# The up projection of a ConvFFN by Strassen's scheme, and its down projection as a pass of its own

## The chip, the cores and the metric

The kernel runs on one core of one Trainium2 chip. The metric is the device time of one launch in microseconds (us). Everything is float32 at the boundary: inputs, outputs and the bytes that move. Most large products are made in three passes of a rounded float32 format (fp32r): a value x is split into a rounded part "hi" and a rest "lo" = x - hi, and a product is w_hi·x_hi + w_hi·x_lo + w_lo·x_hi.

## The reference, cut to what matters

One layer of a hybrid decoder serves a prompt (1024 tokens) and a sample group (8 x 4 = 32 tokens), together T = 1056 columns. The part that changes is the last one, the ConvFFN, with D_MODEL = 1024, D_FF = 2816 and a causal depthwise convolution of width 3:

```
x1 = _layer_norm(DN_ALPHA * x + mix, p['ln1_g'], p['ln1_b'])
h, ffn_state = _causal_dwconv(ffn_prev, x1 @ p['w_up'], p['ffn_dw_w'], p['ffn_dw_b'])
hg, hv = jnp.split(h, 2, axis=-1)
f = (jax.nn.silu(hg) * hv) @ p['w_down']
y = _layer_norm(DN_ALPHA * x1 + f, p['ln2_g'], p['ln2_b'])
```

w_up is 1024 x 5632, w_down is 2816 x 1024. The 5632 up columns are 22 gate tiles and 22 value tiles of 128; gate tile q and value tile q make a pair and give inner tile q (128 of the 2816 inner rows). The outputs are y and the last rows that each convolution and cache has to keep.

## The kernel before, in words

Five engines run programs written out by hand, with semaphores between them: TensorE (PE), VectorE (DVE), ScalarE (ACT), GpSimd (POOL) and SyncE (SP, which only issues DMAs). Nothing is scheduled by a planner: the order of the lines in each engine's block is the order of its work.

In the ConvFFN, channels lie on partitions and the 1056 tokens are columns. The tokens x1 stand split in `x1h` and `x1l` (eight tiles of 128 channels). One weight block, 1024 x 128 of w_up or 256 x 512 of w_down, is 512 KB; it goes through a ring: SP loads it into `wraw`, ACT copies it to `whi` rounded (line 1274), POOL makes `wlo` = raw - hi (line 1482), PE uses both. POOL writes 128x1024 per block.

A pair needs two up products. Each one (`product`, line 2197) runs over 8 channel tiles, 3 passes and 3 chunks of 352 tokens: 72 matmuls of 352 columns, all with a weight load of their own, into three PSUM banks (`psa` for the gate, `psb` for the value). ACT copies the sum to SBUF (`ueg`, `uev`, line 1308) and makes four small copies for the 32 sample tokens. DVE convolves (`ffn_conv`): one tensor_scalar and two scalar_tensor_tensor over 1024 prompt columns (lines 2087 and 2090), the same over 32 sample columns. ACT applies SiLU, DVE multiplies (line 2099), ACT and DVE split the inner tile into `fh`, `fl` (lines 1320 and 2105).

The down projection is woven in: after the two up products of a pair, PE takes half of the down columns of the two inner tiles made before (`down`, line 2856): 4 groups of 18 matmuls of 352 columns. DVE adds each group to the residual in SBUF (`down_add`, line 2119), reading PSUM. So 21 pairs of the 22 follow one another, two to a loop step. The last two inner tiles are multiplied the other way round, with the tokens as the stationary operand and 512 down columns moving (line 2900), which gives y with tokens on partitions; the residual is added there by transposes on PE (line 2887), and DVE, ACT and POOL normalise the rows.

Other names: `res` is x1 in full precision; `stg`, `tmp`, `g_ext`, `zbuf` belong to earlier stages and appear below only as examples of an operation.

Of the kernel before, what the change touches and what calls it, by code (L numbers as in the profile page):

```python
# [24 lines left out]
P = 128  # L25
D = 1024
# [36 lines left out]
def program(nc, A, O):  # L63
    ctx = ExitStack()
    with ctx:
# [72 lines left out]
        psx = [ctx.enter_context(nc.psum_tensor(f"ps{n}", [P, 3, 512], F32)) for n in "ab"]  # L138
# [16 lines left out]
        wm_d = dram("wm_d", [D, D])  # L155

# [47 lines left out]
        rr = at("rr", [P, 8], F32, Z + 29856)  # L204
# [58 lines left out]
        fh = [at(f"fh{j}", [P, 2, T], F32R, X0 + 3 * XB + j * 8448) for j in range(2)]  # L263
        fl = [at(f"fl{j}", [P, 2, T], F32R, X0 + 3 * XB + 16896 + j * 8448) for j in range(2)]
# [6 lines left out]
        yrow = [at(f"yrow{j}", [P, D], F32, X0 + XB + j * 4096) for j in range(4)]  # L271
        fout = at("fout", [P, SG + 1, P], F32, U0)
# [12 lines left out]
        x_in = [sem(f"x_rows_in{j}") for j in range(4)]  # L285
# [26 lines left out]
        ga_in = [sem(f"gate_a_in{j}") for j in range(2)]  # L312
        ma_out = [sem(f"merged_a_out{j}") for j in range(2)]
# [9 lines left out]
        orow_out = [sem(f"latent_rows_out{j}") for j in range(2)]  # L323
# [7 lines left out]
        rr_done = sem("row_sum_inverted")  # L331
# [14 lines left out]
        ql_t = sem("w_uk_transposed")  # L346
        ql_r = sem("w_uk_read")
# [42 lines left out]
        l1_a = sem("residual_scaled")  # L390
# [4 lines left out]
        fh_done = sem("ffn_inner_hi_done")  # L395
        fl_done = sem("ffn_inner_lo_done")
        dn_done = sem("down_tile_done")
# [46 lines left out]
        GATE0, VAL0, DOWN0, GATE1, VAL1, DOWN1 = range(6)  # L444
        NG = FT // 2
        PAIRS = (NG - 1) // 2
        assert NG % 2 == 1

        def kinds(g):
            return (GATE0, VAL0, GATE1, VAL1) if g == "first" else (DOWN0, DOWN1) if g == "last" else range(6)  # L450

        def blk(g, kind):

            if g in ("first", "last"):
                n = (N5 if g == "first" else N5 + 4 + 6 * (NG - 1)) + list(kinds(g)).index(kind)
                return n, n
            n = N5 + 4 + kind + 6 * g[1]
            return 12 * g[0] + n, n

        def acc5(g, kind, q, mm=0):  # L460

            if g == "first":
                return U5[q] + (kind == GATE1 or kind == VAL1)
            if g == "last":
                return U5[q] + 2 + 6 * (NG - 1) + (2 if kind == DOWN1 else 0) + mm // 2
            k = {GATE0: 0, VAL0: 0, DOWN0: 1, GATE1: 3, VAL1: 3, DOWN1: 4}[kind] + mm // 2
            return 12 * g[0] + (U5[q] + 2 + 6 * g[1] + k)

        def inner(g, kind):

            t = 1 if kind in (GATE1, VAL1) else 0
            return (t if g == "first" else 4 * g[0] + (2 + 2 * g[1] + t)), t
# [19 lines left out]
        def count(names):  # L492
# [12 lines left out]
                   + " ".join(" ".join(f"h{c}{k}" for k in range(MT)) + f" x{c}5 x{c}7" for c in (1, 2)))  # L505
        PS = count("m0 t0 m1 t1 t2")
        GS = count(" ".join(f"x{c}1 l{c}1 x{c}3 l{c}3 l{c}5 l{c}7" for c in range(3)))
        part3 = lambda c: slice(c * CH, (c + 1) * CH)

        Y_TURN = (0, 1, 2, 3, 4, 5, 6, 7, 8)  # L510
        Y_BY_VECTOR = (8,)
        YV = count(" ".join(f"s{t}0 s{t}1 v{t} a{t} r{t}" + (f" b{t}" if t in Y_BY_VECTOR else "") for t in Y_TURN))

        def y_half(i, n, h):
            b = i % 4
            if b == 1:
# [33 lines left out]
        def _(sp):  # L550
# [148 lines left out]
            def ffn_load(g, kind):  # L699
                n, ns = blk(g, kind)  # L700
                sp.wait_ge(lo_done, n + 1)
                if kind in (DOWN0, DOWN1):
                    cols = slice(0, D // 2) if kind == DOWN0 else slice(D // 2, D)
                    rows_ = slice(FT - 2, FT) if g == "last" else bass.ds(g[0] * 4 + 2 * g[1], 2)
                    dst = wraw[:, ns % RAW, :].rearrange("p (k c) -> p k c", k=2)
                    sp.dma_start(dst, w_dn_v[:, rows_, cols]).then_inc(raw_in[ns % RAW], 16)
                else:
                    t = kind in (GATE1, VAL1)
                    c = (P if t else 0) + (F if kind in (VAL0, VAL1) else 0)
                    cols = slice(c, c + P) if g == "first" else bass.ds(g[0] * (4 * P) + (c + 2 * P * (1 + g[1])), P)  # L710
                    sp.dma_start(slot3(wraw, ns), w_up_v[:, :, cols]).then_inc(raw_in[ns % RAW], 16)

            for kind in (GATE1, VAL1):
                ffn_load("first", kind)
            with sp.Fori(0, PAIRS) as i:
                for s in range(2):
                    for kind in range(6):
                        ffn_load((i, s), kind)
            for kind in kinds("last"):
                ffn_load("last", kind)  # L720
            sp.wait_ge(h_chain, 12 * FT + 12)
            sp.wait_ge(se_set, 2 * FT)
            sp.dma_start(g2[:, :], A["ln2_g"].to_broadcast([P, D])).then_inc(gb2_in, 16)
            sp.dma_start(b2[:, :], A["ln2_b"].to_broadcast([P, D])).then_inc(gb2_in, 16)
            sp.dma_start(O["conv_s"][0, :, 0:HALO - NT, :], A["state_conv"][0, :, NT:, :]).then_inc(out_s, 16)

            for g in range(SG):
                sp.wait_ge(kf_r, 1 if g < 4 else 2)
                sp.dma_start(state_rows_of(O["ffn_s"][0], g), fout[0:srows(g), g, :]).then_inc(ffn_out, 16)
            sp.dma_start(O["ffn_p"][0, 0].rearrange("t (f p) -> f t p", p=P), fout[0:2 * FT * (FW - 1), SG, :]  # L730
                         ).then_inc(ffn_out, 16)
# [2233 lines left out]
```

## Time and profile before

| | |
|---|---|
| runs | 2050.41, 2047.93 and 2049.80 us, median 2049.8 |
| profiled execution, first to last instruction (span) | 2046.5 us |
| PE busy | 2006.5 us, 98% |
| DVE, ACT, POOL busy | 60%, 35%, 28% |
| granted TensorE clock | 0.997 of 2.4 GHz on average |
| bytes moved | 182.45 MB, 89 GB/s over the span |

The profile gives the span of its execution and not its whole time; the 3.3 us between the span and the median of the runs lie around the instructions. Matmul durations in the rows are latencies that overlap: what a matmul costs is the distance from its start to the next one's start. The ConvFFN begins at about 1254 us and ends with the span.

### The profile page before, as it was taken

To read this page: it belongs to the slowest core of one execution; us is meant where nothing else is said; L and a number is where in the kernel's file an instruction comes from. 1 tells how busy PE (TensorE), PEld (TensorE's weight loads), DVE (VectorE), ACT (ScalarE), POOL (GpSimd) and SP (SyncE) were. 2 spreads that over 40 slices of the span, in tenths; PEclk is the share of its full clock that TensorE was granted. 3 is DMA by queue.
4 is the path that set the end of the run, shared out by engine and by line. 5 is a ranking of instruction groups with operands and counts; after the bars stand their busy time and mean duration, and the time that the engine had idled before them with its cause. 6 is when DMAs were issued, how large, how long until landed. Compare 5 with 4: busy or idle time off the path is not lost.

```text
span 2046.5 us, 33717 instructions
## 1 busy us (share of the span) xinstructions
PE 2006.5 (98%) x13380; PEld 1905.5 (93%) x13380; DVE 1228.7 (60%) x1686; ACT 706.4 (35%) x1175; POOL 564.4 (28%) x284
## 2 busy tenths in 40 slices
PE   8999999999999999989999999999999999999998
PEld 8999999999988999866669998999999999999996
DVE  3999999946755666545453237754545454545447
ACT  4222222226237677653342114322222222222223
POOL 4712444302101010134302256222221212222224
PEclk9999999999999999999999999999999999999999
DMA  6422233215420000166534422111111111111103
GB/s 222 151 94 69 88 95 114 83 53 195 134 74 23 16 23 7 63 233 265 224 148 135 137 90 63 52 46 48 35 58 32 52 42 52 42 52 42 52 31 130
DMA packets 157662, 182.45 MB, mean 89 GB/s; under 512 B 13518, under 2 KB 130528, under 8 KB 153422
## 3 DMA queue, kind: packets, MB, share of 16 engines
q1 hardware_dynamic: 139744, 107.90, 17.3%
q0 software_dynamic: 8320, 46.27, 5.8%
q10 hardware_dynamic: 9469, 26.36, 3.4%
q8 instruction: 106, 1.74, 0.4%
q14 instruction: 23, 0.18, 0.0%
HBM read 149.43 MB, written 31.93 MB: 89 GB/s over the span
## 4 chain that ended last, share of the span: by engine, by line
PE 90%; DVE 5%; ACT 2%; issue 1%; ACTq 0%; DMA 0%; POOL 0%; DVEq 0%
PE psb L2197 28%; PE psa L2197 28%; PE psb L2856 6%; PE psa L2856 6%; PE psb L2390 4%; PE psa L2390 4%; PE pst L2469 1%; PE psb L2657 1%; PE pst L2636 1%; PE psa L2604 1%; PE psb L2604 1%; PE pst L2639 1%; PE psa L2206 1%; PE psb L2343 1%; PE psa L2900 1%
## 5 line engine op out<-in xcount | busy, mean ns | idle before, releaser
L1482 POOL TENSOR_TENSOR wlo<-wraw,whi 128x1024 fp32r<-128x1024 f32 x64 | 172.6, 2710 | 561.5 <-ACT whi L1274 561.5
L1584 DVE SCALAR_TENSOR_TENSOR pst<-g_ext,wtap,pst 128x512 f32<-128x512 f32 x464 | 306.9, 748 | 0.0
L1352 POOL TENSOR_TENSOR wlo<-wraw,whi 128x1024 fp32r<-128x1024 f32 x64 | 154.9, 2425 | 381.5 <-ACT whi L756 286.6
L2087 DVE TENSOR_SCALAR hg<-ueg,fwv,vec 128x1024 f32<-128x1024 f32 x22 | 20.7, 940 | 229.6 <-ACT ueg L1308 225.3
L2197 PE MATMUL psa<-x1h,whi 128*128 128x352 f32 x504 | 109.1, 324 | 0.0
L2197 PE MATMUL psb<-x1h,whi 128*128 128x352 f32 x504 | 109.0, 324 | 0.0
L2197 PE MATMUL psb<-x1h,wlo 128*128 128x352 f32 x504 | 108.6, 323 | 0.0
L2197 PE MATMUL psa<-x1h,wlo 128*128 128x352 f32 x504 | 108.6, 323 | 0.0
L2197 PE MATMUL psb<-x1l,whi 128*128 128x352 f32 x504 | 108.5, 323 | 0.0
L2197 PE MATMUL psa<-x1l,whi 128*128 128x352 f32 x504 | 108.5, 323 | 0.0
L2090 DVE SCALAR_TENSOR_TENSOR hg<-ueg,fwv,hg 128x1024 f32<-128x1024 f32 x44 | 96.9, 2203 | 5.7 <-DVE hg L2087 0.2
L1308 ACT ACTIVATE ueg<-psa 128x1056 f32<-128x1056 f32 x22 | 23.2, 1053 | 219.1 <-PE psa L2197 216.2
L2197 PE MATMUL psa<-xh,whi 128*128 128x352 f32 x432 | 93.6, 325 | 1.2 <-ACT stat L850 1.2
L2197 PE MATMUL psb<-xh,whi 128*128 128x352 f32 x432 | 93.6, 325 | 0.0
L2197 PE MATMUL psb<-xh,wlo 128*128 128x352 f32 x432 | 93.1, 323 | 0.0
L2197 PE MATMUL psa<-xh,wlo 128*128 128x352 f32 x432 | 93.1, 323 | 0.0
L2197 PE MATMUL psa<-xl,whi 128*128 128x352 f32 x432 | 93.0, 323 | 0.0
L2197 PE MATMUL psb<-xl,whi 128*128 128x352 f32 x432 | 93.0, 323 | 0.0
L1428 POOL TENSOR_TENSOR wlo<-wraw,whi 128x1024 fp32r<-128x1024 f32 (+1 forms) x12 | 24.2, 2032 | 245.9 <-ACT whi L934 245.9
L2197 PEld LDWEIGHTS psb<-x1h,wlo 128*128 128x128 f32 x504 | 86.6, 188 | 0.0
L2197 PEld LDWEIGHTS psa<-x1h,wlo 128*128 128x128 f32 x504 | 86.5, 188 | 0.0
L2197 PEld LDWEIGHTS psa<-x1h,whi 128*128 128x128 f32 x504 | 85.8, 189 | 0.3 <-issue 0.3
(550 smaller groups left out, 5249.3 us busy)
## 6 DMA issues: line engine op xcount, KB each, us to landing
wraw<-in_w_up SPq DMA_DIRECT2D x44, 512.0 KB, 3.7
wraw<-in_w_in SPq DMA_DIRECT2D x37, 512.0 KB, 3.8
wraw<-in_w_down SPq DMA_DIRECT2D x22, 512.0 KB, 3.2
xt_d<-tmp POOLq DMA_DIRECT2D x8, 528.0 KB, 3.5
gb_d<-stg ACTq DMA_DIRECT2D x8, 528.0 KB, 2.6
ga_d<-stg ACTq DMA_DIRECT2D x8, 528.0 KB, 3.9
ma_d<-stg ACTq DMA_DIRECT2D x8, 528.0 KB, 2.9
tmp<-gb_d SPq DMA_DIRECT2D x8, 528.0 KB, 3.8
```

Source lines behind the costliest of these rows:

```text
L1308: nc.scalar.activation(split(ue[v][:, FW - 1:]), acc(v), ACT.Copy).then_inc(free[v], 1)
L1352: nc.gpsimd.tensor_tensor(wlo[:, n % HL, :], wraw[:, n % RAW, :], whi[:, n % HL, :].bitcast(F32), ALU.subtract).then_inc(lo_done, 1)
L1428: nc.gpsimd.tensor_tensor(wlo[:, n % HL, 0:w], wraw[:, v, 0:w], whi[:, n % HL, 0:w].bitcast(F32), ALU.subtract).then_inc(lo_done, 1 + s)
L1482: nc.gpsimd.tensor_tensor(wlo[:, (ns + 2) % HL, :], wraw[:, (ns + 2) % RAW, :], whi[:, (ns + 2) % HL, :].bitcast(F32), ALU.subtract).then_ ...
L1584: half[x] = link(nc.vector.scalar_tensor_tensor(out=dst, in0=src, scalar=tap(k_), in1=pst[:, x, :], op0=ALU.mult, op1=ALU.add))
L2087: nc.vector.tensor_scalar(h, src, tap(0), bias, ALU.mult, ALU.add).then_inc(h_chain, 1)
L2090: nc.vector.scalar_tensor_tensor(out=h, in0=src, scalar=tap(k), in1=h, op0=ALU.mult, op1=ALU.add).then_inc(h_chain, 1)
L2197: last = nc.tensor.matmul(out[:, c, 0:CH], w[:, k, :], x[:, k, c * CH:(c + 1) * CH], start=(k == 0 and x is hi_x and w is wh), stop=(k == ...
L2206: last = nc.tensor.matmul(psx[0][:, c, 0:CH], w[:, k, :], x[:, k, part3(c)], start=(k == 0 and x is xh and w is wh), stop=(k == KT - 1 and ...
L2390: r = nc.tensor.matmul(out, w, x, start=first and k == 0, stop=last and k == len(steps) - 1)
L2604: last = nc.tensor.transpose(dst[:, k, v * P:(v + 1) * P], cb[j][:, 4 * g + v, k * P:(k + 1) * P], ident[:, :])
L2856: last = nc.tensor.matmul(psx[q][:, c, 0:CH], w[:, k, cols], x[:, k, c * CH:(c + 1) * CH], start=k == 0 and w is wh and x is fh[p_], stop= ...
```

## The change: what it does

**Up projection.** Pairs 0 and 1 stay as they were. For the other 20 pairs the product of a pair is taken as a 2 x 2 block product: channels in a lower and an upper half (4 tiles each), tokens in a left and a right half (528 each), and as the other side the gate and the value tile. Strassen's scheme in Winograd's form makes it with 7 block products instead of 8, from sums of weight blocks and sums of token blocks:

- Token sums: four blocks of 128 x 4 x 528, made once before pair 2, by DVE (`token_sum`, 8 instructions of 128x1056), split by ACT (`token_high`, 8), DVE and POOL (`token_low`, 4 each). Two of them overwrite `res`, which is first stored to DRAM (`xr_d`, 4.3 MB); DVE's first token sum waits for that store.
- Weight sums: POOL makes four of 128x512 per pair (`up_sum`); ACT and POOL split seven blocks of 128x512 per pair (`up_high`, `up_low`). Raw weights lie in two buffers of four blocks; `whi` and `wlo` have one slot of 512 columns for each of the seven.
- Products: per pair 7 groups of 24 matmuls of 264 columns (`up_product`), into a ring of four places of two PSUM banks. A product waits until the product four before it has been read.
- Results: ACT copies the first product (`first_part`), DVE makes seven additions of 128x528, each of one product in PSUM and one operand in SBUF (`up_add`), and writes gate and value halves straight into `ueg` and `uev`. The big copies of ACT are gone.

**Down projection.** The finished inner tiles go to DRAM (`f_d`). After the last up product, three rounds over the tokens (tiles 0, 1 and the sample; 2 to 4; 5 to 7) run over all 22 inner tiles with the tokens stationary and 512 down columns moving, all by `down_step`; the y rows stay in PSUM for the round. w_down is loaded and split again in every round (66 blocks of 128x1024). The 32 sample tokens are multiplied unsplit in plain float32, four products side by side in four column groups (`sample_step`, 11 times). The convolution of the last pair and its product lie on DVE in the first round. The loops of the ConvFFN are written out.

The core of the diff ("..." where it is cut):

```
-            def ffn_hi(g, kind):
...
+            def up_sum(i, s, out, a, b, op):
+                pool.wait_ge(raw_in[i % 2], UP_IN0 + 64 * (i // 2 + 1))
+                pool.wait_ge(up_s, 4 * i + s - 1)
+                nc.gpsimd.tensor_tensor(out, a, b, op).then_inc(up_s, 1)
+
+            def up_low(i, e):
+                pool.wait_ge(hi_done, UP_HI0 + 7 * i + e + 1)
+                src = sums[:, :] if e == 3 else up_raw(i)[:, (0, 1, 0, None, 2, 1, 3)[e], :]
+                nc.gpsimd.tensor_tensor(wl8[:, UP_SLOT[e], :], src, wh8[:, UP_SLOT[e], :].bitcast(F32), ALU.subtract
+                                        ).then_inc(lo_done, 1)
...
+            def token_sum(n):
+                if n != 1:
+                    dve.wait_ge(xr_out, 32)
...
+                    nc.vector.tensor_tensor(t_sum[n][:, ks, :], a[:, ks, :], b[:, ks, :], ALU.subtract).then_inc(l1_v, 1)
...
+            token_sum(0)
+            token_sum(1)
+            conv(0, 0)
+            token_sum(3)
+            token_sum(2)
+            token_low(0)
+            conv(0, 1)
+            inner(0)
+            token_low(2)
+            for i in range(NP):
+                conv(i + 1, 0)
+                gate_left(i)
+                conv(i + 1, 1, i)
+                inner(i + 1)
+                with_fifth(i)
+                with_seventh(i)
+                value_right(i)
+                if i == NP - 1:
+                    for x in range(4):
+                        inner_low(x)
+                gate_right(i)
+                value_left(i)
+            residual_scale(0)
...
+            def up_product(i, e, dst, hi_x, lo_x):
+                wh, wl = entry(wh8, e), entry(wl8, e)
+                pe.wait_ge(lo_done, UP_LO0 + 7 * i + e + 1)
+                for k in range(HK):
+                    for w, x in ((wh, hi_x), (wh, lo_x), (wl, hi_x)):
+                        for c in range(2):
+                            last = nc.tensor.matmul(dst[:, c, :], w[:, k, :], x[:, k, c * QF:(c + 1) * QF],
+                                                    start=k == 0 and w is wh and x is hi_x,
+                                                    stop=k == HK - 1 and w is wl)
+                last.then_inc(w_used, 1)
...
+            def down_step(r, t, k, hs=(0, 1), stop=False):
...
+                for f, w in ((x1h, whi), (x1h, wlo), (x1l, whi)):
+                    for h in hs:
+                        last = nc.tensor.matmul(y_half(t, h), f[:, x % FR, cols], w[:, s, h * 512:(h + 1) * 512],
+                                                start=False, stop=stop and f is x1l)
```

Where instructions move on DVE: in the steady part, before, the end of a pair, behind the value convolution (`hv` and `hg` are the convolved tiles, `uev` the value tile, `sev` its sample part, `psa` and `psb` PSUM).

```order
L2119 TENSOR_TENSOR res<-res,psb 128x1056
L2098 REGISTER_ALU
L2099 TENSOR_TENSOR hv<-hg,hv 128x1056
L2114 REGISTER_ALU
L2119 TENSOR_TENSOR res<-res,psa 128x1056
L2105 TENSOR_TENSOR fl_198<-hv,fh_196 128x1056
L2116 REGISTER_ALU
L2119 TENSOR_TENSOR res<-res,psb 128x1056
```

In the changed kernel DVE from the value convolution of one of the 20 Strassen pairs to the pair's end (`ps6` and `pst` are PSUM, `u1`, `u3` and `inr` hold partial sums in SBUF).

```order
L2317 TENSOR_SCALAR hv_201<-uev_199,fwv_54,vec_52 128x1024
L2320 SCALAR_TENSOR_TENSOR hv_201<-uev_199,fwv_54,hv_201 128x1024
L2338 TENSOR_TENSOR u1_210<-ps6,u1_210 128x528
L2320 SCALAR_TENSOR_TENSOR hv_201<-uev_199,fwv_54,hv_201 128x1024
L2317 TENSOR_SCALAR hv_201<-sev_203,fwv_54,vec_52 128x32
L2320 SCALAR_TENSOR_TENSOR hv_201<-sev_203,fwv_54,hv_201 128x32 x2
L2328 TENSOR_TENSOR hv_201<-hg_200,hv_201 128x1056
L2338 TENSOR_TENSOR u3_211<-pst,u1_210 128x528
L2338 TENSOR_TENSOR inr_197<-ps6,u1_210 128x528
L2338 TENSOR_TENSOR uev_199<-pst,inr_197 128x528
L2338 TENSOR_TENSOR ueg_198<-ps6,u3_211 128x528
L2338 TENSOR_TENSOR uev_199<-ps6,inr_197 128x528
```

The four additions of down groups and the split of the inner tile have left the pair; seven additions of half the width have come in, five of them at its end, where the third of these five frees the PSUM place that PE's next pair begins with.

POOL before, for three blocks of the ring (a pair takes three: gate, value, down):

```order
L1482 TENSOR_TENSOR wlo_60<-wraw_58,whi_59 128x1024
L1481 REGISTER_ALU
L1482 TENSOR_TENSOR wlo_60<-wraw_58,whi_59 128x1024
L1481 REGISTER_ALU
L1482 TENSOR_TENSOR wlo_60<-wraw_58,whi_59 128x1024
```

POOL in the changed kernel, one pair (the raw weights of every other pair lie in `x1f`):

```order
L1681 TENSOR_TENSOR sums_209<-x1f_196 128x512
L1686 TENSOR_TENSOR wlo_60<-x1f_196,whi_59 128x512
L1681 TENSOR_TENSOR x1f_196<-x1f_196 128x512
L1686 TENSOR_TENSOR wlo_60<-x1f_196,whi_59 128x512
L1681 TENSOR_TENSOR x1f_196<-sums_209,x1f_196 128x512
L1686 TENSOR_TENSOR wlo_60<-x1f_196,whi_59 128x512
L1686 TENSOR_TENSOR wlo_60<-sums_209,whi_59 128x512
L1681 TENSOR_TENSOR x1f_196<-x1f_196 128x512
L1686 TENSOR_TENSOR wlo_60<-x1f_196,whi_59 128x512 x3
```

Three instructions of 128x1024 per pair have become eleven of 128x512.

## Rows read from the trace of the kernel before

**Rows 1.** The page, busy time, share of the span, instructions.
```profile
PE 2006.5 (98%) x13380; PEld 1905.5 (93%) x13380; DVE 1228.7 (60%) x1686; ACT 706.4 (35%) x1175; POOL 564.4 (28%) x284
```
**Rows 2.** The page, the chain that ended last, by engine.
```profile
PE 90%; DVE 5%; ACT 2%; issue 1%; ACTq 0%; DMA 0%; POOL 0%; DVEq 0%
```
**Rows 3.** The chain in order of time: start us, us, what.
```profile
1281.30 11.88 PE psa L2197 x72
...
1747.66 2.91 PE psa L2856 x18
```
**Rows 4.** Timeline of PE, start and duration us: 512 columns, then 256.
```profile
599.28 0.39 PE L2390 MATMUL psa<-ckvh,wlo 128*128 128x512 f32 x1
...
601.36 0.39 PE L2390 MATMUL psa<-ckvh,wlo 128*128 128x512 f32 x1
...
606.01 0.28 PE L2390 MATMUL psb<-whi,ckvl 128*128 128x256 f32 x1
...
607.08 0.28 PE L2390 MATMUL psb<-whi,ckvl 128*128 128x256 f32 x1
```
**Rows 5.** Timeline of PE: plain float32 in four column groups; transposes.
```profile
922.85 1.92 PE L2636 MATMUL pst<-ct,qc 128*32 128x512 f32 x16
...
2004.64 0.60 PE L2887 MATMUL psa<-ident,res 128*128 128x128 f32 x4
2005.00 0.48 PE L2900 MATMUL psa<-whi,fh 128*128 128x512 f32 x1
```
**Rows 6.** One pair of the steady part: us, busy us of each engine, clock, DMA.
```profile
1339.79:1374.74 34.95, 34.95 (x218) 34.95 (x217) 17.20 (x18) 8.12 (x16) 8.12 (x4) 1.00 0.15 46
```
**Rows 7.** Timeline of DVE, start and duration us, one value convolution and what follows.
```profile
1539.18 0.81 DVE L2087 TENSOR_SCALAR hv<-uev,fwv,vec 128x1024 f32<-128x1024 f32 x1 [5.15 <-ACT uev L1308]
1540.12 1.28 DVE L2090 SCALAR_TENSOR_TENSOR hv<-uev,fwv,hv 128x1024 f32<-128x1024 f32 x1
1541.32 1.25 DVE L2119 TENSOR_TENSOR res<-res,psa 128x1056 f32<-128x1056 f32 x1
1542.49 1.28 DVE L2090 SCALAR_TENSOR_TENSOR hv<-uev,fwv,hv 128x1024 f32<-128x1024 f32 x1
1543.68 0.29 DVE L2087 TENSOR_SCALAR hv<-sev,fwv,vec 128x32 f32<-128x32 f32 x1
1544.01 0.54 DVE L2090 SCALAR_TENSOR_TENSOR hv<-sev,fwv,hv 128x32 f32<-128x32 f32 x2
1544.47 1.25 DVE L2119 TENSOR_TENSOR res<-res,psb 128x1056 f32<-128x1056 f32 x1
1545.63 1.25 DVE L2099 TENSOR_TENSOR hv<-hg,hv 128x1056 f32<-128x1056 f32 x1
1546.80 1.25 DVE L2119 TENSOR_TENSOR res<-res,psa 128x1056 f32<-128x1056 f32 x1
```
**Rows 8.** Timelines of DVE and POOL where both work.
```profile
1528.63 4.62 DVE L2090 SCALAR_TENSOR_TENSOR hg<-ueg,fwv,hg 128x1024 f32<-128x1024 f32 x2
...
1528.89 3.27 POOL L1482 TENSOR_TENSOR wlo<-wraw,whi 128x1024 fp32r<-128x1024 f32 x1 [9.93 <-ACT whi L1274]
```
**Rows 9.** Single lines of DVE: duration ns min/median/max.
```profile
L2090 DVE SCALAR_TENSOR_TENSOR hg<-ueg,fwv,hg x44: 1283/1286/3298, 1282.5 to 1984.5; 128x1024 f32<-128x1024 f32 x44
...
L2119 DVE TENSOR_TENSOR res<-res,psb x40: 1246/1252/1255, 1334.7 to 2004.1; 128x1056 f32<-128x1056 f32 x40
...
L1563 DVE COPY gs_ext<-g_ext x8: 181/181/2341, 49.2 to 379.2; 128x32 f32<-128x32 f32 x8
```
**Rows 10.** Groups of POOL's instructions, one of 512 columns: busy us, mean ns.
```profile
L1428 POOL TENSOR_TENSOR wlo<-wraw,whi 128x512 fp32r<-128x512 f32 x4 | 5.2, 1297 | 0.0
```
**Rows 11.** DMA issues of an earlier stage: KB each, us to landing.
```profile
zbuf<-z_d SPq DMA_DIRECT2D x1, 2640.0 KB, 12.4
```
**Rows 12.** Timelines of POOL and PE: last split before pair 1; last matmul.
```profile
1276.73 2.80 POOL L1500 TENSOR_TENSOR x1l<-res,x1h 128x352 fp32r<-128x352 f32 x3
...
2037.45 0.40 PE L2900 MATMUL psa<-whi,fl 128*32 128x512 f32 x1
```

More of the change, by code:

```diff
@@ L439, in program, with wait_used @@
         U5 = list(uses)
[L444 to L472, printed above, removed]
+        Y_END = (4, 12)
+        def wait_used(eng, x):
+            r, k = (x - 1) // FT, (x - 1) % FT
+            if k == FT - 1:
+                eng.wait_ge(y_t, Y_END[r])
+            else:
+                eng.wait_ge(w_used, DN_P0 + r * (FT - 1) + k + 1)
+        up_block = lambda q, v: N5 + 2 * q + v
+        up_free = lambda q, v: U5[v] + q
         w_in_v = A["w_in"].rearrange("l (k p) c -> p (l k) c", p=P)
@@ L713, in _ @@
[L713 to L731, printed above, removed]
@@ L1322, in _ @@
-            act_ffn("first")
-            with act.Fori(0, PAIRS) as i:
-                for s in range(2):
-                    act_ffn((i, s))
+            hi(up_block(1, 1))
+            for k in (0, 2, 4, 6):
+                act.wait_ge(l1_v, VS[f"l2{k}"])
+                step(f"z{k}", nc.scalar.activation(res[:, k, :], res[:, k, :], ACT.Identity,
+                                                   bias=vec[:, V_L1B + k:V_L1B + k + 1]))
+            act.wait_ge(l1_s, AS["z6"])
+            act.wait_ge(l1_g, GS["l27"])
@@ L1346, in _ @@
+            for i in (6, 7, 8):
+                y_scale(i)
         @block.gpsimd
@@ L1525, in _ @@
+            for i in (6, 7):
+                y_bias(i)
         @block.vector
@@ L2091, in ffn_conv, with inner @@
                                                            op1=ALU.add).then_inc(h_chain, 1)
-                        if v and g != "first" and part_ == 0 and k == 1:
-                            down_add(g, DOWN0 if kind == VAL0 else DOWN1, 0)
-            def ffn_mult(g, kind):
-                q, t = inner(g, kind)
+                        if between is not None and part_ == 0 and k == 1:
+                            first_and_sixth(between)
+            def inner(q):
                 dve.wait_ge(si_done, q + 1)
@@ L2807, in first_up @@
             def first_up():
-                blocks = [blk("first", kind) for kind in (GATE0, VAL0)]
+                blocks = [(up_block(0, v), up_block(0, v)) for v in range(2)]
                 for c in range(3):
```

814 lines of the change are left out of this document (544 added, 270 removed).

## The prediction, made before the changed kernel was run
> **What bounds the kernel now.** I read the page first: PE is busy 98% of the span, no other engine over 60% [rows 1], and the chain that ended last runs through PE for 90% [rows 2]. The chain in order of time then shows the ConvFFN as products end to end: 72 matmuls in 11.65 to 11.88 us, 18 in 2.91 [rows 3]. One pair lasts 34.95 us, PE busy for all of it, DVE 17.20, ACT 8.12, POOL 8.12, granted clock 1.00, so the 2.4 GHz level [rows 6]. So PE's matmul starts are the time today, and what counts is whether they still are once the pair is short.
>
> **What PE gains.** The cost of a matmul is the distance of starts. For 512 columns that is (601.36 - 599.28) / 9 = 0.231 us, for 256 it is (607.08 - 606.01) / 9 = 0.119 [rows 4]; the line between them gives 0.161 for 352 columns, and 34.95 / 216 = 0.162 is what a pair shows [rows 6]. So 264 columns cost 0.1225 by the line; the block products change bank at every matmul, as the 352 ones do, and those lie 1 ns over it: I take 0.124 (bounds 0.119 and 0.130). A Strassen pair is 7 x 24 = 168 matmuls, 20.8 us (20.0 to 21.8), where the two products took 144 x 0.162 = 23.3. On PE alone that is 2.5 us a pair, 50 us for 20 pairs.
>
> **The down projection changes little.** Before: 20 pairs x (34.95 - 23.3) = 233 us woven in, and from 2003.9, where the last group ends, to the last matmul's end at 2037.85 another 34 [rows 5, 12]: 267 us. After: 8 whole token tiles x 22 x 3 x 2 = 1056 matmuls of 512 columns at 0.232 are 245; 64 transposes at 0.36 for four [rows 5] are 5.8, and 0.6 for eight first matmuls behind them; the sample is 11 groups of four plain float32 matmuls side by side, of which two took 1.92 us [rows 5], so 10.6; its end and the turned state rows about 3.4. Together 265 us. The second half of the question is therefore DVE, POOL and the two seams.
>
> **DVE and POOL in a steady pair.** DVE's own work, start to start [rows 7]: a convolution 0.94 + 1.20 + 1.19 + 0.33 + 0.46 = 4.12, two of them 8.24, the product of the inner tile 1.17, and seven additions of 528 columns. The addition of 1056 costs 1.17; half of that and the fixed part is 0.62, seven are 4.3. Sum 13.7 us, well under 20.8. POOL: eleven instructions of 512 columns at 1.30 [rows 10], 14.3 us, also under.
>
> But the two don't run freely beside each other. In [rows 8] two scalar_tensor_tensor took 4.62 us instead of the 2.48 that they take alone, while POOL's split between them took 3.27. The longest of their kind took 3298 ns where the median is 1286 [rows 9]: the first ran through, POOL stood until it was done, then the second stood until POOL was done. They take turns, whole instruction by whole instruction. The additions that read PSUM are never touched: 40 of them lie between 1246 and 1255 ns [rows 9], though POOL splits three blocks in every pair [rows 6]. A copy of 32 columns, 181 ns, was held for 2341 [rows 9], so small ones stand in the queue as well.
>
> In a Strassen pair DVE has 13 instructions that read SBUF alone: per convolution one tensor_scalar and two scalar_tensor_tensor of 1024 columns and the same three of 32, and the product. POOL has eleven, and before it had three. As long as POOL has work, DVE waits before each of its 13 for one of POOL's, 1.30 less the 0.2 to 0.3 that an instruction needs to begin anyway: about 1.04. Some of POOL's eleven pass under additions or while DVE waits for PE. I count ten that are waited for: 13.7 + 10.4 = 24.1 us. With eight it is 22.0, with eleven 25.1. PE cannot run ahead, since its next pair begins in the place that DVE's fifth-last work frees (`value_right`), behind all 13. So the pair is the longer of 20.8 and this sum. I take 23.5, a little under 24.1, for the chances of POOL to slip through; range 20.8 to 25.1. That is the size of the 23.3 that it replaces: the gain of PE goes into turns at the port.
>
> The Trainium skill, page "SBUF — State Buffer", section "Who interferes with whom", puts it as an exclusive lock: a DVE instruction with two SBUF inputs, or a two-port mode, and a GpSimd instruction that reads SBUF block each other for the whole instruction, PSUM readers are free. This trace agrees as far as it goes (3298 against 1286 ns, and 1255 at most for PSUM readers); that it also holds for scalar_tensor_tensor of 32 columns no row shows. By the rule the pair is 24.1; if only those four small ones of a pair were free it would be about 21, which is the second case below.
>
> **The seam at the start.** Up to the end of pair 1's product nothing is moved, except four small ACT additions: it ends at 1304.8 (two products behind 1281.30 [rows 3]). The store of `res`, 4.3 MB, can be issued after POOL's last split at 1279.5 [rows 12], some 3 us later with ACT's work. A load of 2.64 MB took 12.4 us [rows 11]; at that rate 4.3 MB take 20 us; nothing else of size moves then, so I take 16, landed at 1299 (1294 to 1304). From there DVE must do, before the second Strassen pair can begin: eight token sums and four splits of 1056 columns (12 x 1.17 = 14.0), four convolutions (16.5), two products (2.3), five additions (3.1): 36 us. POOL has 11 + 11 small ones and four splits of 1056 columns in that time, and about 20 of DVE's 40 turns are lost to them: 21 us. So the second Strassen pair begins at 1299 + 36 + 21 = 1356, say 1355. On PE's account it would be 1304.8 + 20.8 = 1325.6. The seam costs 29 us (10 if DVE never waits for POOL, 34 if the store is late).
>
> **The seam in the middle and the end.** After the last block product DVE has four splits of inner tiles, two additions and the residual scaling (2304 columns, 1.8 us) before PE's first transposes: 5 us if PE was the slower, 8 if DVE was. In round 0 PE needs 3.25 us a step, POOL's split of 1024 columns 2.4, and DVE's last pair is still to be convolved between them: another 4 us. The tail behind the last matmul was 8.65 us; the last tile now has 128 rows and not 32, so 0.7 more for its store.
>
> **The sum** (places on the scale of the profiled execution, whose own time before is its span of 2046.5 and some 3.3 us around it, which makes the median 2049.8): 1355 + 18 x 23.5 + 20.8 for the last pair = 1798.8; + 8 + 4 + 265 + 9.35 = 2085.2, and 3.3 around it: 2088.5, say 2088 us, 38 over the median of 2049.8, slower by 1.9%. Against the span before, by parts: the first Strassen pair takes 50.2 us for 23.3 (+ 26.9), 18 pairs + 3.6, the last - 2.5, the middle + 12, the down pass - 2, the tail + 0.7: + 38.7. Nothing of PE's 50 us arrives.
>
> **Rivals.**
>
> *PE sets the pair.* The small instructions don't queue, or POOL's work falls into DVE's waits for PE. For it: POOL is released product by product, since each slot of `whi` is free only when PE has used it, so it is not always backed up; and both sums alone (13.7 and 14.3) leave room. Against: 13.7 + 14.3 = 28 less the 4.3 of additions is 23.7 of work that takes turns, more than 20.8. Then 1351 + 19 x 20.8 = 1746, + 5 + 1 + 265 + 9.35 + 3.3 = 2030, faster by 1%. Between it and the forecast lies everything from eight turns down. The point at which it changes sign: equal time at a pair of (2049.8 - 2088.5) / 18 + 23.5 = 21.35 us.
>
> *The turns cost nothing at the start either.* The store lands early and DVE goes through in 36 us: 1336 + 395 + 5 + 265 + 9.35 + 3.3 = 2014. Against: [rows 8], which show the turns plainly.
>
> *Worse than turns.* PE stands 2.7 us a pair; should its granted clock fall to the lower level in these stands (the trace has no stand of that length inside the ConvFFN to read it from), a product of 3.0 us would take up to 5.9, and pairs come to 25 or 26: 18 x 2 us more, 2125. The same comes of it if the first round of the down pass goes at the pace of POOL's turns (2.4 + 1.2 against 3.25, 22 times) together with a late store.
>
> *Matmuls of 264 columns don't cost what the line says* (a floor near 0.140): a pair is 23.5 on PE as well. Against: 256 columns already show 0.119. It would only leave the forecast as it is.
>
> **How the numbers follow.** DVE and POOL set the pair: 0.60, of its own 2065 to 2115. PE sets it: 0.22, 2022 to 2045. Free at the start too: 0.06. Worse: 0.12. A difference under 0.2% (4 us) is about what this measurement can't tell from none. Faster: 0.22 less a little at its slow edge, 0.06, and a small part of the first case with eight turns or fewer: 0.28. Slower 0.68, same 0.04. The range from 2030 to 2120 leaves out the 0.06, half of the second case and a third of the worst.
>
> **What would show it.** Right: starts of 264-column matmuls 0.124 apart inside a block product, but block products of a pair spread over 23 to 25 us, the idle time of PE before the pair's first product put down to DVE; scalar_tensor_tensor of 1024 columns at 2.3 us in the mean and the small ones at 1 us and more; POOL's 512-column instructions over 1.3. The second Strassen pair near 1355, and the wait before the first pair's second product put down to ACT behind DVE's token sums. Wrong: pairs of 20.8 us with PE without a gap, or DVE's small instructions still at 0.25 us; a down pass that is far from 265 us would be a fault of another step.

## Result, and the profile after

The changed kernel takes 2094.5 us (median of 4 runs, 2093.8 to 2096.5), the kernel before 2048.9 (4 runs, 2047.7 to 2050.4): ratio 1.022, 95% interval 1.0207 to 1.0233, slower. The forecast was 2088.

The page of the changed kernel, busy times and the chain by engine, against [rows 1, 2]:

```profile
PE 1983.1 (95%) x13460; PEld 1823.8 (87%) x13460; DVE 1451.0 (69%) x1800; ACT 788.0 (38%) x1355; POOL 929.2 (44%) x511
...
PE 65%; DVE 24%; issue 5%; ACT 3%; DMA 2%; ACTq 0%; SPq 0%; POOL 0%; DVEq 0%
```

DVE has 24% of the chain where it had 5. PE is less busy in a longer span, so it waits.

Stretches of the changed kernel, columns as in [rows 6]: Strassen pairs 2 to 4, one in which PE never stands (its next pair begins at 1571.22, 0.2 us before the stretch ends), the last pair, and the wait behind it.

```profile
1361.20:1385.80 24.60, 20.72 (x168) 20.50 (x168) 23.79 (x21) 7.05 (x18) 22.88 (x15) 1.00 0.21 65
1385.85:1408.46 22.61, 22.32 (x168) 22.10 (x169) 22.15 (x21) 6.98 (x17) 17.25 (x11) 0.92 0.23 71
1408.46:1432.00 23.54, 20.87 (x169) 20.65 (x169) 23.09 (x21) 6.98 (x17) 17.74 (x11) 1.00 0.22 69
1547.86:1571.40 23.54, 23.54 (x170) 23.54 (x171) 22.42 (x21) 7.36 (x21) 16.63 (x11) 0.87 0.22 70
1780.45:1801.30 20.85, 20.85 (x168) 20.63 (x168) 18.71 (x20) 5.31 (x13) 6.18 (x3) 1.00 0.21 68
1801.30:1811.10 9.80, 0.00 (x0) 0.00 (x0) 4.29 (x7) 1.78 (x5) 0.00 (x0) 0.60 0.88 260
```

PE's part of a pair is 20.85 us, as the last pair shows, in which it doesn't wait. The pairs before it last 22.6 to 24.6; from 1361.23 to 1780.45 lie 18 of them, 23.29 us each. DVE is busy for nearly all of each.

One value convolution and the end of a pair on DVE, against [rows 7]:

```profile
1556.76 0.71 DVE L2338 TENSOR_TENSOR ueg<-pst,u 128x528 f32<-128x528 f32 x1 [0.66 <-PE pst L3127]
...
1558.22 2.20 DVE L2320 SCALAR_TENSOR_TENSOR hv<-uev,fwv,hv 128x1024 f32<-128x1024 f32 x1
1560.35 0.69 DVE L2338 TENSOR_TENSOR u<-ps,u 128x528 f32<-128x528 f32 x1
1560.96 1.70 DVE L2320 SCALAR_TENSOR_TENSOR hv<-uev,fwv,hv 128x1024 f32<-128x1024 f32 x1
1562.59 1.27 DVE L2317 TENSOR_SCALAR hv<-sev,fwv,vec 128x32 f32<-128x32 f32 x1
1563.90 2.49 DVE L2320 SCALAR_TENSOR_TENSOR hv<-sev,fwv,hv 128x32 f32<-128x32 f32 x2
1566.49 2.28 DVE L2328 TENSOR_TENSOR hv<-hg,hv 128x1056 f32<-128x1056 f32 x1
```

POOL in the same microseconds:

```profile
1562.38 1.45 POOL L1686 TENSOR_TENSOR wlo<-wraw,whi 128x512 fp32r<-128x512 f32 x1 [0.79 <-ACT whi L1374]
1563.79 1.30 POOL L1686 TENSOR_TENSOR wlo<-sums,whi 128x512 fp32r<-128x512 f32 x1
1565.05 1.29 POOL L1681 TENSOR_TENSOR wraw<-wraw 128x512 f32<-128x512 f32 x1
1566.36 1.29 POOL L1686 TENSOR_TENSOR wlo<-wraw,whi 128x512 fp32r<-128x512 f32 x1
```

Read the two together. Three instructions of 32 columns, 0.29, 0.25 and 0.25 us alone, take 1.27 and, two of them together, 2.49. The first ends at 1563.86 and the last at 1566.39, each just behind the end of a POOL instruction (1563.83 and 1566.34); the row merges the last two, so the end between them isn't seen. The addition, which reads PSUM, takes 0.69 as if POOL weren't there.

The same by groups, DVE and then POOL in 1385 to 1700 (busy us, mean ns of one, idle before):

```profile
L2320 DVE SCALAR_TENSOR_TENSOR hg<-ueg,fwv,hg 128x1024 f32<-128x1024 f32 x28 | 61.8, 2207 | 1.0
L2320 DVE SCALAR_TENSOR_TENSOR hv<-uev,fwv,hv 128x1024 f32<-128x1024 f32 x27 | 42.0, 1556 | 0.5
L2320 DVE SCALAR_TENSOR_TENSOR hg<-seg,fwv,hg 128x32 f32<-128x32 f32 x28 | 32.4, 1156 | 1.0
L2320 DVE SCALAR_TENSOR_TENSOR hv<-sev,fwv,hv 128x32 f32<-128x32 f32 x26 | 31.8, 1225 | 0.9
L2328 DVE TENSOR_TENSOR hv<-hg,hv 128x1056 f32<-128x1056 f32 x13 | 25.1, 1930 | 1.4
L2317 DVE TENSOR_SCALAR hv<-sev,fwv,vec 128x32 f32<-128x32 f32 x13 | 16.6, 1280 | 0.0
L2317 DVE TENSOR_SCALAR hv<-uev,fwv,vec 128x1024 f32<-128x1024 f32 x14 | 16.3, 1164 | 0.0
L2317 DVE TENSOR_SCALAR hg<-seg,fwv,vec 128x32 f32<-128x32 f32 x14 | 15.9, 1134 | 0.0
...
L2338 DVE TENSOR_TENSOR ueg<-ps,u 128x528 f32<-128x528 f32 x21 | 14.7, 698 | 0.6 <-PE ps L3127 0.6
...
L1686 POOL TENSOR_TENSOR wlo<-x1f,whi 128x512 fp32r<-128x512 f32 x42 | 65.9, 1573 | 40.6 <-ACT whi L1374 40.4
```

Less their own length (1.286, 0.81, 1.25; 0.29 and 0.25 for the small ones) a pair holds this much waiting: large scalar_tensor_tensor 2 x 0.92 + 2 x 0.27, large tensor_scalar 0.35, product 0.68, small ones 2 x 0.91 + 2 x 0.98 + 0.99 + 0.84. That is 3.4 us in the large and 5.6 in the six small, 9.0 together; 13.7 + 9.0 = 22.7, and 0.6 is left for gaps between starts. DVE hardly waits for PE: once for 0.66 us (the first row above) and once for 0.56 in all the pairs of that stretch.

### The profile page after: what moved, and what is told of

It reads as the page before. It is cut to its first block, busy times and chain, and to the rows that moved or that the text cites. A ratio compares the mean times of both kernels' runs of the same rounds, so it can differ in the third digit from the quotient of the medians.

```text
span 2093.0 us, 34337 instructions
## 1 busy us (share of the span) xinstructions
PE 1983.1 (95%) x13460; PEld 1823.8 (87%) x13460; DVE 1451.0 (69%) x1800; ACT 788.0 (38%) x1355; POOL 929.2 (44%) x511
## 4 chain that ended last, share of the span: by engine, by line
PE 65%; DVE 24%; issue 5%; ACT 3%; DMA 2%; ACTq 0%; SPq 0%; POOL 0%; DVEq 0%
PE ps L2472 31%; PE ps L2665 9%; PE ps L3194 8%; DVE hv L2320 6%; DVE hg L2320 5%; PE pst L3194 3%; DVE hv L2317 2%; PE ps L2879 2%; DVE hg L2317 2%; PE pst L2744 1%; PE ps L2932 1%; PE pst L2911 1%; DVE u L2338 1%; DVE ueg L2338 1%; PE ps L3127 1%
## 5 line engine op out<-in xcount | busy, mean ns | idle before, releaser
L1532 POOL TENSOR_TENSOR wlo<-wraw,whi 128x1024 fp32r<-128x1024 f32 x66 | 161.4, 2451 | 386.7 <-ACT whi L859 291.8
L2472 PE MATMUL ps<-xh,whi 128*128 128x352 f32 x864 | 187.2, 325 | 1.2 <-ACT stat L953 1.2
L2472 PE MATMUL ps<-xh,wlo 128*128 128x352 f32 x864 | 186.2, 323 | 0.0
L2472 PE MATMUL ps<-xl,whi 128*128 128x352 f32 x864 | 186.0, 323 | 0.0
L2472 PEld LDWEIGHTS ps<-xh,whi 128*128 128x128 f32 x864 | 147.0, 189 | 1.9 <-issue 1.8
L2472 PEld LDWEIGHTS ps<-xh,wlo 128*128 128x128 f32 x864 | 148.3, 188 | 0.0
L2472 PEld LDWEIGHTS ps<-xl,whi 128*128 128x128 f32 x864 | 146.7, 188 | 0.0
L1735 POOL TENSOR_TENSOR wlo<-pieces,whi 128x1024 fp32r<-128x1024 f32 x44 | 109.7, 2498 | 79.0 <-ACT whi L1418 78.8
L1686 POOL TENSOR_TENSOR wlo<-wraw,whi 128x512 fp32r<-128x512 f32 x60 | 95.8, 1600 | 54.9 <-ACT whi L1374 54.8
L1686 POOL TENSOR_TENSOR wlo<-x1f,whi 128x512 fp32r<-128x512 f32 x60 | 96.9, 1620 | 52.4 <-ACT whi L1374 52.2
L859 ACT ACTIVATE whi<-wraw 128x1024 fp32r<-128x1024 f32 x34 | 35.8, 1056 | 125.8 <-DMA wraw<-wm_d 61.4
```

The costliest lines, as they stand in the source:

```text
L1532: nc.gpsimd.tensor_tensor(wlo[:, n % HL, :], wraw[:, n % RAW, :], whi[:, n % HL, :].bitcast(F32), ALU.subtract).then_inc(lo_done, 1)
L1686: nc.gpsimd.tensor_tensor(wl8[:, UP_SLOT[e], :], src, wh8[:, UP_SLOT[e], :].bitcast(F32), ALU.subtract).then_inc(lo_done, 1)
L1735: nc.gpsimd.tensor_tensor(two(wlo[:, s, :]), down_raw(d), two(whi[:, s, :].bitcast(F32)), ALU.subtract).then_inc(lo_done, 1)
L2472: last = nc.tensor.matmul(out[:, c, 0:CH], w[:, k, :], x[:, k, c * CH:(c + 1) * CH], start=(k == 0 and x is hi_x and w is wh), stop=(k == ...
```

## Experiments

In all of these "before" is the kernel before, run beside them (medians 2049.6 and 2050.2 us). The changed kernel wasn't run again; where a time is compared with its 2094.5, the two were measured apart.

### Shorter instructions on POOL

```
-                nc.gpsimd.tensor_tensor(out, a, b, op).then_inc(up_s, 1)
+                h = slice(0, 256 if i else 512)
+                nc.gpsimd.tensor_tensor(out[:, h], a[:, h], b[:, h], op).then_inc(up_s, 1)
...
-                nc.gpsimd.tensor_tensor(wl8[:, UP_SLOT[e], :], src, wh8[:, UP_SLOT[e], :].bitcast(F32), ALU.subtract
+                h = slice(0, 256 if i else 512)
+                nc.gpsimd.tensor_tensor(wl8[:, UP_SLOT[e], h], src[:, h], wh8[:, UP_SLOT[e], h].bitcast(F32), ALU.subtract
```

> From the second Strassen pair on, POOL's eleven instructions of a pair take 256 columns and not 512 (the other half of the weight sums and low parts is left out, so the up products are made with stale low parts there). Theory (DVE takes turns with POOL and sets the pair): a turn costs the length of one POOL instruction, 0.65 us in place of 1.30 (half, an estimate from the 512-column one), less the 0.25 that a start needs anyway, so nine waits fall from 1.04 to about 0.4 each, DVE's pair from 23.3 to 13.7 + 3.6 = 17.3 us, and PE sets the pair at 20.8: 18 x 2.5 = 45 us less, 2049. Rival (DVE's own work and its dependencies, ACT, the clock or PE itself set the pair): nothing changes, 2094.

Measured 2043.8 us (6 runs), ratio to before 0.997 (0.9958 to 0.9982). One pair:

```profile
1479.40:1500.00 20.60, 20.60 (x171) 20.60 (x170) 16.01 (x20) 6.76 (x17) 11.30 (x12) 1.00 0.26 79
```

PE stands no more from the second Strassen pair to the end of the last, and nothing was changed on PE or DVE. The time is 5 us under the expected 2049, since a pair is 20.6 us and not 20.8. So the length of POOL's instructions is what lengthens the pair. That POOL itself was late (the products also wait for its low parts) isn't excluded by this run; the next two exclude it.

### Shorter additions on DVE

```
-                nc.vector.tensor_tensor(out, up_bank(i, e), in1, ALU.add).then_inc(mg_done, 1)
+                c = slice(0, QF // 2 if i else QF)
+                nc.vector.tensor_tensor(out[:, :, c], up_bank(i, e)[:, :, c], in1[:, :, c], ALU.add).then_inc(mg_done, 1)
```

> From the second Strassen pair on, DVE's seven additions of a pair take the first half of their columns, 264 of 528 (the other half is left out). They read PSUM and never waited for POOL. Theory (DVE's chain, own work plus turns, sets the pair): an addition falls from 0.62 to 0.35 start to start, seven give 1.9 us, so the pair falls from 23.3 to 21.4 and the time by 18 x 1.9 = 34 us to 2060; a little less if POOL then meets DVE's next instruction instead of an addition. Rival (what both engines hold exclusively is full: DVE's 9.4 us of instructions on SBUF alone and POOL's 14.3 make 23.7, which is the pair): the additions lie beside POOL's work, nothing changes, 2094. Rival (PE or its clock sets the pair): nothing changes either.

Measured 2064.9 us (4 runs), ratio 1.0069 (1.0053 to 1.0085): 29.6 under the changed kernel. Two pairs:

```profile
1441.90:1485.40 43.50, 41.57 (x339) 41.13 (x338) 42.59 (x41) 13.60 (x34) 35.85 (x23) 1.00 0.24 75
```

A pair is 21.75 us. The additions gave back 7 x 0.27 = 1.9, the pair shrank by 1.5, and the time stayed 5 us above the expected 2060. So DVE's chain sets the pair, and the rival that the two engines' exclusive time is simply full falls: it left the additions without effect. Most likely the missing 0.4 went into more waiting for POOL: the waits, added up as above, are 9.6 us for 9.0 (the large scalar_tensor_tensor of the value takes 2092 ns in the mean for 1556, that of the gate 1741 for 2207).

### The six small instructions through PSUM

```
+                h_m = h_s
+                if 1 <= q <= NP:
+                    e = 3 if v else 1
+                    h_m = p_bank[(7 * (q - 1) + e) % 4][:, 0, QF:QF + NS].rearrange("p (b t) -> p b t", t=NT)
...
+                        if h_m is not h_s:
+                            dve.wait_ge(w_used, UP_P0 + 7 * (q - 1) + e + 1)
...
-                        h = h_s if part_ else h_p
+                        h, to = (h_m, h_s if k == FW - 1 else h_m) if part_ else (h_p, h_p)
```

(`h_m` lies in unused columns of the PSUM place of product 1 or 3, which is finished then and which DVE itself has yet to read.)

> The six instructions of 32 columns of a pair (sample part of both convolutions) keep their intermediate result in a PSUM bank whose product is finished and not yet read, so that each reads or writes PSUM. Nothing is left out. Theory with small instructions queuing: the nine microseconds of waiting in a pair are 5.6 in the six small ones and 3.5 in the large ones by their mean durations; without the 5.6 DVE's pair is 17.7 us and PE sets it at 20.8: 45 us less, 2049. Rival (what both engines hold exclusively is full): 23.7 less the 1.6 of own work of the small ones is 22.1, 18 x 1.2 = 21 us less, 2073. Rival (POOL's instruction is only met by the next large one instead): 2094.

Measured 2043.9 us (7 runs), ratio 0.9973 (0.9961 to 0.9984). One pair:

```profile
1475.30:1495.90 20.60, 20.60 (x171) 20.60 (x170) 18.35 (x22) 6.19 (x17) 19.81 (x12) 1.00 0.25 79
```

Small instructions of its steady part by groups (busy us, mean ns of one, idle before):

```profile
L2323 DVE TENSOR_SCALAR ps<-seg,fwv,vec 128x32 f32<-128x32 f32 x12 | 3.8, 314 | 8.4 <-ACT kfs L1387 8.4
...
L2326 DVE SCALAR_TENSOR_TENSOR ps<-seg,fwv,ps 128x32 f32<-128x32 f32 x12 | 3.1, 256 | 0.4
L2326 DVE SCALAR_TENSOR_TENSOR hg<-seg,fwv,ps 128x32 f32<-128x32 f32 x12 | 3.0, 248 | 0.4
```

The last of these still writes SBUF and reads one SBUF tile beside PSUM; at 248 ns it waits for nobody. The small ones moved 32 columns and cost 5.6 us of a pair. The large ones still wait, and a little longer: added up as above their waits are 4.1 us a pair for 3.4 (the value's scalar_tensor_tensor takes 1945 ns for 1556), so the rival that POOL only meets the next large one is right in a small part. It no longer matters, since 13.7 + 4.1 is under PE's 20.6. Now POOL is the one that is held (19.81 busy of 20.60, 17.7 before), PE is never. With POOL's eleven instructions at full width the pair is PE's, as with half of them: POOL was not late by itself.

### DVE's queue behind the store, at the start

```
+            conv(0, 0)
+            conv(0, 1)
+            inner(0)
             token_sum(0)
             token_sum(1)
-            conv(0, 0)
             token_sum(3)
             token_sum(2)
             token_low(0)
-            conv(0, 1)
-            inner(0)
             token_low(2)
```

(ACT's `silu(0)` and copies of pair 1 are moved forward to match.)

> Only the start seam: DVE does both convolutions and the inner product of pair 0 before the token sums, while it waits for the store of the residual; ACT puts the silu of pair 0 and the copies of pair 1 earlier. Nothing is left out. Theory (the seam is DVE's queue behind the store): 9.4 us of own work and about two turns leave the path from the store's landing at 1300 to the second Strassen pair at 1361, which then begins near 1350: 11 us less, 2083. Rival (POOL's chain behind the weights that land at 1300.7, 22 instructions of 512 columns and four of 1056, sets it, 22 x 1.3 + 4 x 2.4 = 38 us and the waits): at most 3 us less, 2091.

Measured 2086.9 us (5 runs), ratio 1.0176 (1.0162 to 1.0191): 7.6 less. The second pair begins at 1350.39, as expected, while the span is 2085.1 and not 2082; from that pair to the end the profiled execution has 734.7 us where the changed kernel had 731.8. Read from the starts on DVE and PE, 1.4 of those 3 us lie in the next 18 pairs, 1.0 in the last pair with the wait behind it, 0.5 in the down pass; no run says why.

Start of the seam, PE in the changed kernel (start, duration, idle time before and what ended it):

```profile
1320.19 0.81 PE L3127 MATMUL ps<-x1h,whi 128*128 128x264 f32 x2 [7.88 <-ACT ueg L1393]
1333.76 1.22 PE L3127 MATMUL ps<-tfr,whi 128*128 128x264 f32 x4 [8.09 <-ACT uev L1393]
1350.49 0.81 PE L3127 MATMUL ps<-x1h,whi 128*128 128x264 f32 x2 [5.38 <-DVE ueg L2338]
1361.23 0.51 PE L3127 MATMUL ps<-x1h,whi 128*128 128x264 f32 x2 [2.17 <-DVE uev L2338]
```

The same in this run:

```profile
1321.41 1.22 PE L3127 MATMUL ps<-tfr,whi 128*128 128x264 f32 x4 [5.13 <-POOL wlo L1686]
...
1339.66 0.81 PE L3127 MATMUL ps<-x1h,whi 128*128 128x264 f32 x2 [6.96 <-DVE ueg L2338]
1350.39 0.51 PE L3127 MATMUL ps<-x1h,whi 128*128 128x264 f32 x2 [2.36 <-DVE uev L2338]
```

The two waits for ACT, whose copy stood behind DVE's convolution, which stood behind the store, are gone; in place of one of them PE waits 5.13 us for POOL.

### The store in quarters

```
+                    to_dram(lowk, left, xq_out[0])
...
-            for cols in (left, right):
-                act.dma_start(xr_d[:, :, cols].rearrange("k p n -> p k n"), res[:, :, cols]).then_inc(xr_out, 16)
...
+            to_dram(highk, left, xq_out[1])
+            to_dram(lowk, right, xq_out[2])
+            to_dram(highk, right, xr_out)
...
-                if n != 1:
-                    dve.wait_ge(xr_out, 32)
+                if n == 1:
+                    dve.wait_ge(l1_s, AS["z6"])
+                else:
+                    dve.wait_ge(xq_out[{0: 0, 3: 1, 2: 2}[n]], 16)
```

(The first cut stands in ACT's block, the last in `token_sum`. DVE's queue is reordered as the expectation says, and some of ACT's splits of weights move back.)

> The start seam again, now with the store of the residual cut in four quarters, each token sum waiting only for the quarter that it overwrites, and DVE in the order: gate convolution of pair 0, sums 0 and 1, value convolution and inner product, sums 3 and 2, splits. Nothing is left out. With the whole store awaited, the reordered queue brought the second Strassen pair from 1361 to 1350. Theory (DVE's queue behind the store): sums 0 and 1, 8 us in that run with POOL beside them, now lie before 1300, where POOL is idle; the pair begins near 1343, time 2078 to 2080. Rival (POOL, which has no idle time between 1300 and 1350 and whose weights land at 1300 as before, sets the seam): nothing beyond the reordered queue, 1350, 2087.

Measured 2077.9 us (4 runs), ratio 1.0131 (1.0116 to 1.0147). DVE at the seam, changed kernel:

```profile
1300.08 3.53 DVE L2286 TENSOR_TENSOR res<-res 128x1056 f32<-128x1056 f32 x2 [21.15 <-DMA xr_d<-res]
```

and here:

```profile
1288.96 2.42 DVE L2299 TENSOR_TENSOR res<-res 128x1056 f32<-128x1056 f32 x2
1291.30 3.52 DVE L2299 TENSOR_TENSOR tf<-res 128x1056 f32<-128x1056 f32 x2
```

The first sum starts 11 us earlier and the second Strassen pair at 1345.29, 16 us earlier. POOL gets its first weights at 1290.94 for 1300.76: their load had shared the transfer engines with the whole store (12.9 us to landing), now with little more than its first quarter (3.9). Neither expectation for this run had that. How much of the 16 us is the earlier store and how much the earlier weights, this run doesn't tell.

### SyncE's queue in the middle

```
+                if i == NP - 1:
+                    for x in range(4):
+                        inner_load(x)
+                    residual_load(0)
+                    inner_load(4)
                 inner_out(i + 1)
 
-            for x in range(4):
-                inner_load(x)
-            inner_load(4)
-            residual_load(0)
```

> Only SyncE's queue at the middle seam: the loads of the first five stored inner tiles and of the residual for round 0 are issued ahead of the store of the inner tile that DVE finishes last in the last Strassen pair. Nothing is left out. Theory (the 9.8 us in which PE waits for the scaled residual are a queue on SyncE: its loads stand behind a store that waits for DVE's last inner product): the residual is there when DVE has made its last addition, the wait falls to 3 or 4 us (two additions, the scaling 1.4), 6 us less: 2088. Rival (the rate of the transfers, 0.88 of the engines' time there, or DVE's own work sets the wait): at most 1 us less, 2093.

Measured 2088.5 us (5 runs), ratio 1.0187 (1.0173 to 1.0201): 6.0 less. SyncE's queue in the changed kernel:

```profile
1797.60 0.33 SPq L757 DMA_DIRECT2D f_d<-hv  x1
1798.03 5.45 SPq L781 DMA_DIRECT2D inr<-f_d  x10
1803.57 1.00 SPq L790 DMA_DIRECT2D rr<-xr_d  x2
```

and in this run:

```profile
1785.24 3.65 SPq L781 DMA_DIRECT2D inr<-f_d  x8
1791.10 0.99 SPq L790 DMA_DIRECT2D rr<-xr_d  x2
...
1799.05 0.32 SPq L757 DMA_DIRECT2D f_d<-hv  x1
```

The residual is fetched 12 us earlier, and DVE's scaling now follows its last addition (1803.55, no idle time before it). PE's wait for it, 9.84 us in the changed kernel, is here:

```profile
1805.05 1.94 PE L3185 MATMUL ps<-ident,rr 128*128 128x128 f32 x8 [2.34 <-DVE rr L2372]
```

The wait lost 7.5 us and the time 6.0, since PE worked 22.2 us on the last pair for 20.85, with a granted clock of 0.92 in it for 1.00. The transfers were not too slow; they stood behind a store that waited for DVE's last inner product.

### The three together

> The three edits together: sample parts of the convolutions through PSUM in the steady pairs, the split store and reordered queues at the start, the early loads in the middle. Nothing is left out. If each seam is its own place the gains add: 2044 for the steady pairs alone, 14 less for the start (in the first pair the small instructions no longer queue either), 6 less in the middle: 2024, 1.2% under the kernel before. If PE's gain at the start is taken back by POOL, 2031; if the middle is bound by transfers, 2030 to 2037.

Measured 2024.7 us (4 runs), ratio to before 0.9873 (0.9858 to 0.9888). One pair:

```profile
1458.30:1478.90 20.60, 20.60 (x171) 20.60 (x170) 16.13 (x21) 6.19 (x17) 19.81 (x12) 1.00 0.27 85
```

PE where the second Strassen pair begins, and the down pass:

```profile
1338.91 0.51 PE L3147 MATMUL ps<-x1h,whi 128*128 128x264 f32 x2 [0.61 <-DVE uev L2358]
...
1737.63 1.94 PE L3204 MATMUL ps<-ident,rr 128*128 128x128 f32 x8 [5.72 <-DVE rr L2391]
```

It beats both kernels: 25 us under the one before, which took 2050.2 beside it, and 70 under the changed one. The gains nearly add: one by one they were 50.6, 16.6 and 6.0, which makes 73.2, and together they are 69.8. The expectation had left out 2.6 us of it for the start: in the first Strassen pair small instructions still queue in the run with the split store (two of them take 3.56 us), and no longer once they go through PSUM, so that part is in both single gains.

## Why the prediction was right, step by step

Terms of the sum, predicted and read from the changed kernel: second Strassen pair begins 1355 / 1361.2; 18 pairs 423 / 419.2; last pair 20.8 / 20.85; wait in the middle 8 / 9.8; down pass with round 0's extra 269 / 273.8; tail 9.35 / 8.1; around the span 3.3 / 1.5. Sum 2088.5 / 2094.5. The miss of 6.0 is a sum of both signs, + 6.2, - 3.8, + 0.1, + 1.8, + 4.8, - 1.3 and - 1.8, so part of its smallness is luck. The last term compares a median with the span of one execution; in each single run on record the two differ by 1.7 to 2.2 us.

**Matmuls of 264 columns.** Right: 20.85 us in the last pair, 20.60 in steady pairs of the experiments, which is 0.1226 a matmul (the line of [rows 4] gives 0.1225, 0.124 was taken). The fourth rival, a floor near 0.140, is out.

**DVE and POOL take turns.** Right in mechanism and size: 23.29 for 23.5. Shown by taking it away from either side: half the length on POOL, or no SBUF-only operands in six tiny instructions of DVE, and the pair is PE's. The count was ten waits of 1.04; it is 9.0 us in the mean, and 0.6 of gaps that the sum had left out. The sum gave 24.1; the 23.5 was a judgement below it, and that it came within 0.2 is partly luck. The step that no row had shown, that the small scalar_tensor_tensor queue as well, is with the small tensor_scalar the larger part of it, 5.6 of the 9.0. One slip is without effect on the sum: `value_right` is DVE's third-last work of a pair, not its fifth-last; all 13 instructions lie ahead of it either way.

The Trainium skill, page "SBUF — State Buffer", section "Who interferes with whom", was the source for that step, beside the copy of 32 columns in [rows 9]; by its rule an instruction with one input in SBUF and one in PSUM stays out of the lock. The runs agree: 1225 ns in the mean with both in SBUF, 248 with one in PSUM.

**The seam at the start.** Right in kind, 6 us short. The store landed at 1300 (1299 said). From there DVE's chain took 61 us for the 57 worked out (rounded down to 1355). Its turns were priced at POOL's 1.30, though four of POOL's instructions there have 1056 columns. Behind them two of DVE's splits took 6.89 us for 2.3 (DVE, changed kernel; then its scaling in the middle):

```profile
1318.79 6.89 DVE L2292 TENSOR_TENSOR resr<-res,tfr 128x1056 fp32r<-128x1056 f32 x2
...
1809.63 1.36 DVE L2371 TENSOR_SCALAR rr<-rr 128x2304 f32<-128x2304 f32 x1 [3.52 <-DMA rr<-xr_d]
```

Pair 1's product waited 2.55 us on PE as well, since ACT had four additions and two DMA issues ahead of the copy that frees PSUM; not foreseen, but DVE's chain, not PE, sets this seam.

**The seam in the middle.** The size was near, 9.8 for 8, but that is luck, for the cause was for the most part another. The 8 us were to be DVE's own work; with the loads out of the way that costs PE 2.34 us (the run with SyncE's queue reordered). The rest was loads issued behind `inner_out`: ACT's rounding of the inner tiles, which DVE's splits need, waited for them first, and the last 3.5 us before DVE's scaling were a wait for the residual. The scaling itself took 1.36 us where 1.8 was estimated. ACT, changed kernel:

```profile
1801.88 0.92 ACT L1424 ACTIVATE x1h<-inr 128x256 fp32r<-128x256 f32 x2 [8.20 <-DMA inr<-f_d]
```

SyncE's queue was not walked through in the forecast.

**The down pass.** 273.8 us for 265 and 4 of waits in round 0, so 4.8 us short. The sample step was taken from its own duration, 0.96; two steps of 12 matmuls with one sample group take 6.76 us here (PE, changed kernel, two groups in a row):

```profile
1870.26 1.06 PE L3204 MATMUL pst<-pieces,inr 128*32 128x512 f32 x8
1877.02 1.06 PE L3204 MATMUL pst<-pieces,inr 128*32 128x512 f32 x8
```

24 x 0.2325 = 5.58 of it are matmuls, so a group is 1.18, and eleven are 2.4 more. The clock, 0.76 in the pass's first 12 us, behind the 9.8 us in which PE had nothing to do, costs 2.9 (an estimate, 12 x 0.24). The waits of PE for POOL in round 0, put at 4, were 0.54 and 1.87. Together 7.7 of the 8.8 us over 265; the other 1.1 stay open. This is read from the trace alone; no run took these apart.

**The clock.** The rival had it fall in PE's stands and lengthen the pair. It does fall in places, each time behind a stand of 2.5 us or more (0.92 and 0.87 in the stretches above), but such a pair is no longer: 22.6 us from start to start with 0.92, against 23.5 with 1.00, in which PE works 20.87 and stands the rest. Only in two of the 18 pairs, with a granted clock of 0.87, does PE not stand behind its last product. There DVE waits 0.66 and 0.56 us for a product, so PE takes part in setting those two; they last 23.4 and 23.3 us.

**The rival that PE sets the pair** (2030 us) describes what the kernel becomes once the small instructions are out of the queue: 2043.9 with both seams as they are, 2024.7 with them mended. It fails here by six instructions of a quarter microsecond.

## What to carry to other kernels

When work moves from PE to DVE and POOL, count the instructions that use SBUF alone on both, and not only their columns: one that finds the other engine at work waits until the other's instruction is through, here 0.8 to 1.0 us in the mean even for 32 columns. What it waits for is as long as the other engine's instructions are: with these at half length the waiting no longer reached PE. A small operation can be taken out of that queue by keeping one operand in a PSUM place that is finished and not yet read. And walk every queue, SyncE's too, past the new stage: here one store that waited for the end of the stage held back all loads behind it, 12 us in the case of the residual.

## What the runs showed that was not expected

- Freed of six waits, DVE has idle time, and POOL, whose work is unchanged, is busy 19.8 us of 20.6 for 17.7 of 23.5: the waiting moves to the engine that has time for it.
- A load of 1 MB in four parts, begun on another queue 0.4 us behind two stores of 2.1 MB, took as long as they did, 12.9 us from issue to landing in the median; with one quarter of the store ahead of it and the others issued 2.9 us and more after its start, it took 3.9. The load and the stores had nearly the same number of packets (2112 and 2080), the stores' being four times as large: that fits queues which take turns by the packet and not by the byte, but no run here tests it.
- In the changed kernel a lower clock and standing take each other's place: a pair at 0.92 to 0.94 is followed by a stand of 0.2 to 0.5 us, one at 0.98 to 1.00 by 2.5 to 3.9. In the two steady runs in which PE never waits in the pairs (half-length POOL instructions, small ones through PSUM) the clock is 1.00 in every stretch looked at.
